# A three-layer network on one Trainium2 core: modulation, attention masks and forgetting bias moved from TensorE to VectorE

## What is computed

```python
def masked_softmax(s, mask):
    s = jnp.where(mask, s, -jnp.inf); m = max(s); e = where(mask, exp(s - m), 0.0)
    return e / where(sum(e) > 0, sum(e), 1.0)

# layer 0: stick-breaking attention (8 heads) beside sparse attention (8 heads, 2 key groups)
for each query block i of 128:                      # nsa_attention
    pc = masked_softmax(q_i @ kc.T * scale, cmp_end <= tpos)        # 31 compressed keys
    ps = masked_softmax(q_i @ k_slc.T * scale, kpos <= tpos)        # selected keys
    pw = masked_softmax(q_i @ k_win.T * scale, causal, window 512)
    o  = gate0 * pc @ vc + gate1 * ps @ v_slc + gate2 * pw @ v_win

# layer 1: forgetting attention (16 heads)
cum = cumsum(log_sigmoid(f + b_f))
s = q_i @ k.T * scale + (cum[query] - cum[key]);  p = masked_softmax(s, key <= query)

# both layers end with a gated feed-forward
a, b = split(h @ w_in); a = conv3(a) + conv_b; x = x + (silu(a) * b) @ w_out      # 2 x 2816 features

# second network: six modulation vectors for c and for c_ctx
sh1, sc1, g1, sh2, sc2, g2 = split(silu(c) @ ada_w + ada_b, 6)                    # ada_w is 1024 x 6144
csh1, csc1, ...            = split(silu(c_ctx) @ ada_w + ada_b, 6)
h = rmsnorm_2(x, norm1_g) * (1 + sc1) + sh1
# then neighbourhood attention, spatial gating, a merge, a product-key expert layer
```

## Time and profile before

| | before |
|---|---|
| median of 3 runs | 3334.88 us |
| lowest, highest | 3329.38, 3342.94 us |
| the profiled execution | 3336.33 us |
| its span | 3334.9 us |
| its mean granted TensorE clock | 0.968 |
| TensorE busy | 3136.4 us (94% of the span) |
| VectorE busy | 2149.3 us (64%) |
| ScalarE busy | 1283.5 us (38%) |
| GpSimd busy | 810.8 us (24%) |
| HBM read | 476.42 MB |

### The profile page before, as it was taken

The page is one execution under the profiler, slowest core; times in us unless marked ns, Lnnn a source line. Parts: engine busy times, 40 slices in busy tenths (PEclk is TensorE's granted clock), DMA queues, the critical chain, the costliest instruction groups (busy, mean ns, idle before and its releaser), DMA issues. The chain is left out here.

```text
span 3334.9 us, 44712 instructions
## 1 busy us (share of the span) xinstructions
PE 3136.4 (94%) x17144; PEld 2684.2 (80%) x17144; DVE 2149.3 (64%) x4042; ACT 1283.5 (38%) x2260; POOL 810.8 (24%) x708
## 2 busy tenths in 40 slices
PE   7998899999999999997998989888989999999998
PEld 5556678888776788885776768888989999999998
DVE  4464556465566563644334348997878888888886
ACT  3344543233343332333442223338943433333333
POOL 1001110000000300024000023578824333433431
PEclk9799999999999999997998989999999999999999
DMA  3441113222211223221111222454699989999893
GB/s 140 145 159 66 39 64 104 93 95 101 70 52 51 89 91 105 95 95 43 51 61 64 95 76 84 131 192 169 233 331 315 330 307 323 323 325 337 305 327 115
DMA packets 182690, 516.03 MB, mean 155 GB/s; under 512 B 15056, under 2 KB 77520, under 8 KB 177360
## 3 DMA queue, kind: packets, MB, share of 16 engines
q1 hardware_dynamic: 129344, 307.27, 26.9%
q0 software_dynamic: 40464, 160.45, 13.8%
q10 hardware_dynamic: 12672, 45.47, 3.6%
HBM read 476.42 MB, written 36.70 MB: 154 GB/s over the span
## 5 line engine op out<-in xcount | busy, mean ns | idle before, releaser
L238 PE MATMUL bank<-h_hi,w_hi 128*128 128x512 f32 (+1 forms) x2528 | 963.6, 381 | 67.6 <-DVE h_lo L304 13.7
L238 PE MATMUL bank<-h_lo,w_hi 128*128 128x512 f32 (+1 forms) x2528 | 949.7, 376 | 0.0
L212 DVE TENSOR_TENSOR w_lo<-w_raw,w_hi 128x1024 fp32r<-128x1024 f32 (+1 forms) x460 | 590.0, 1283 | 318.5 <-ACT w_hi L206 316.3
L206 ACT ACTIVATE w_hi<-w_raw 128x1024 fp32r<-128x1024 f32 (+1 forms) x508 | 546.0, 1075 | 529.1 <-PE bank L238 511.3
L238 PEld LDWEIGHTS bank<-h_hi,w_hi 128*128 128x128 f32 x2528 | 484.4, 192 | 152.9 <-issue 50.0
L238 PE MATMUL bank<-h_hi,w_lo 128*128 128x512 f32 (+1 forms) x2528 | 596.6, 373 | 9.5 <-POOL w_lo L219 9.5
L238 PEld LDWEIGHTS bank<-h_lo,w_hi 128*128 128x128 f32 x2528 | 485.6, 192 | 65.5 <-issue 10.2
L238 PEld LDWEIGHTS bank<-h_hi,w_lo 128*128 128x128 f32 x2528 | 460.1, 189 | 75.5 <-POOL w_lo L219 10.5
L238 PE MATMUL bank<-e_hi,w_hi 128*128 128x384 f32 x1024 | 345.5, 337 | 9.1 <-DVE e_lo L2369 9.1
L238 PE MATMUL bank<-e_lo,w_hi 128*128 128x384 f32 x1024 | 344.2, 336 | 0.0
L2278 POOL DMA_INDIRECT own_row<-in_u_rows,own_e x128 | 156.8, 1225 | 300.2 <-DVE sums L2406 261.1
(11 more groups left out here) (434 smaller groups left out, 4326.2 us busy)
## 6 DMA issues: line engine op xcount, KB each, us to landing
w_raw<-in_w SPq DMA_DIRECT2D x476, 512.0 KB, 3.8
ada_w<-in_ada_w POOLq DMA_DIRECT2D x24, 1024.0 KB, 5.1
expert_weights<-G ACTq DMA_DIRECT2D x12, 2048.0 KB, 7.2
Gin<-expert_weights SPq DMA_DIRECT2D x32, 768.0 KB, 9.2
w_raw<-in_w SPq DMA_DIRECT2D x32, 704.0 KB, 4.1
hidden_ahead<-u_stage ACTq DMA_DIRECT2D x48, 192.0 KB, 3.0
ahead<-hidden_ahead SPq DMA_DIRECT2D x24, 384.0 KB, 6.5
x<-in_x ACTq DMA_DIRECT2D x4, 512.0 KB, 10.7
```

Source lines behind the costliest of these rows:

```text
L206: sc.activation(w_hi[s][:, 0:n], w_raw[raw_slot[u]][:, 0:n], ACT.Copy).then_inc(*w_hi_made.next(u))
L212: ve.tensor_tensor(w_lo[s][:, 0:n], w_raw[raw_slot[u]][:, 0:n], w_hi[s][:, 0:n], ALU.subtract).then_inc(*w_lo_made.next(u))
L238: m = te.matmul(out, wt, moving, start=(not low and k == 0 and moving is hi), stop=(low and k == len(blocks) - 1))
```

## The change

1. **Modulation** leaves TensorE and the sparse attention. A new function `modulation` is part of each feed-forward layer: 24 tiles of 128 x 1024 of the transposed `ada_w` per layer, fetched by GpSimd (512 KB each, a ring of four), and for each tile two VectorE row products, with silu(c) and with silu(c_ctx), each summed along its row into `mod`. The host lays `ada_w` out by output row, and c and c_ctx as rows repeated over the partitions; ScalarE fetches these (1 MB) and takes their Silu once per layer. In the first half the products begin with the third feature tile, one product ahead of `a_in` and one ahead of `bn`, then one beside each out unit; in the second half all 11 tiles have two. `scaled_g` is made at the end of the second layer.
2. **Masks of the sparse attention.** The mask matmuls are gone. VectorE adds `near` or `cfar` to the scores and takes the minimum in one instruction (`tensor_tensor_reduce`), which writes the masked scores to `Pm`; the exponential reads them there. Scores of slot g wait for that minimum of slot g-1. Transposes are those of slot g-2, VectorE does the reciprocal and scaling of slot g-1 after the minimum of slot g, and the query unit's matmuls stand between scores and transposes.
3. **Bias of the forgetting attention.** The `pick` matmuls are gone. The running sum is written to memory by GpSimd and read back repeated over the partitions, two rows per pair (512 KB, a ring of four `crow`). VectorE adds it and takes the minimum in one instruction; queries carry -scale.

```diff
@@ ffn, vector()
+            products = products_vector()
                     split_lo(ub)
+                    if half or f >= 2:
+                        run(products, 1)
...
                     ve.scalar_tensor_tensor(cv[0][:, :], a_in[:, 2:T + 2], tap[2], cv[1][:, :], ALU.mult, ALU.add).then_inc(*dve.next(name, "conv", half, f))
+                    if half or f >= 2:
+                        run(products, 1)
                     ve.wait_ge(*w_used.at(ub))
@@ modulation, products_vector()
+            ve.wait_ge(*act.at("silu c", layer))
+            for n in tiles:
+                ve.wait_ge(*tile_in[n % RING].at(n))
+                if n - 1 in tiles:
+                    ve.wait_ge(*dve.at("ada first", n - 1))
+                ve.scalar_tensor_tensor(spent[:, :], w[n % RING][:, :], 1.0, silu[:, 0, :], ALU.mult, ALU.mult,
+                                        accum_out=mod[:, n, 0:1]).then_inc(*dve.next("ada first", n))
+                yield
+                ve.wait_ge(*dve.at("ada first", n))
+                ve.scalar_tensor_tensor(w[n % RING][:, :], w[n % RING][:, :], 1.0, silu[:, 1, :], ALU.mult, ALU.mult,
+                                        accum_out=mod[:, n, 1:2]).then_inc(*dve.next("ada", n))
+                yield
@@ nsa, tensor()
                         if g:
-                            te.wait_ge(*act.at("nsa exp", hh, g - 1))
+                            te.wait_ge(*dve.at("nsa least", hh, g - 1))
...
-                        te.matmul(part, ident_r[:, :], mask, start=False, stop=True).then_inc(*pe.next("nsa scores", hh, g))
...
-                if 0 < g <= slots and g % 2 == 0:
-                    ada_turn(g // 2 - 1)
-                for n in range(2) if g == 1 else (g,) if 1 < g < slots else ():
-                    ada_tensor(n)
@@ nsa, vector()
-                        least = ve.tensor_reduce(sm[:, k + 1:k + 2], S[:, 0:w], AX.X, ALU.min)
...
+                        far = cfar[:, i, :] if b == 0 else near[:, T - w:T]
+                        ve.tensor_tensor_reduce(Pm[hh][m % 2][b][:, 0:w], s_bank[hh][:, 0:w], far, 1.0, 1e20,
+                                                ALU.add, ALU.min, sm[:, k + 1:k + 2]).then_inc(*dve.next("nsa least", hh, g))
@@ fox, tensor()
                         if m:
-                            te.wait_ge(*act.at("fx exp", hh, m - 1))
...
-                        te.matmul(S[:, 0:kw], pick[rows, p, :], cum_hi[rows, 0:kw], start=False, stop=False)
-                        te.matmul(S[:, 0:kw], pick[rows, p, :], cum_lo[rows, 0:kw], start=False, stop=True).then_inc(*pe.next("fx scores", hh, m))
+                            te.wait_ge(*dve.at("fx least", hh, m - 1))
@@ fox, vector()
+                        if i == 0:
+                            ve.wait_ge(*crow_in[p % 4].at(p))
                         ve.wait_ge(*dve.here())
-                        row_max(S[:, 0:kw], small[hh][:, c:c + 1], small[hh][:, c + 1:c + 2], SCALE).then_inc(*dve.next("fx max", hh, m))
+                        ve.tensor_tensor_reduce(Pm[hh][m % 2][:, 0:kw], S[:, 0:kw], crow[p % 4][:, hh, 0:kw], 1.0, 3e38,
+                                                ALU.add, ALU.min, small[hh][:, c + 1:c + 2]).then_inc(*dve.next("fx least", hh, m))
@@ fox, gpsimd()
+            gp.wait_ge(*dve.at("fx cum"))
+            gp.dma_start(cum_dram[:, :], cum[0:16, :]).then_inc(*cum_out.next("out"))
+            gp.wait_ge(*cum_out.at("out"))
             for p in range(8):
...
+                if p >= 4:
+                    gp.wait_ge(*dve.at("fx least", 1, 4 * (p - 3) - 1))
+                gp.dma_start(crow[p % 4][:, :, :], cum_dram[2 * p:2 * p + 2, :].unsqueeze(0).to_broadcast([P, 2, T])).then_inc(*crow_in[p % 4].next(p))
```

238 lines of the change are left out of this document (103 added, 135 removed).

## The result

| | before | after |
|---|---|---|
| median, runs | 3336.07 us, 4 | 3253.95 us, 4 |
| lowest, highest | 3329.38, 3342.94 | 3249.13, 3254.31 |
| ratio to before, 95% interval | | 0.9745, 0.9725 to 0.9765 |
| span of the profiled execution | 3334.9 | 3252.7 |
| mean granted TensorE clock | 0.968 | 0.971 |

The account below looks back on a forecast made before the run. TensorE, busy 94% of the span, was taken as the bound. Terms of -52.6 (sparse attention), -10 (forgetting attention) and +6 (feed-forward) sum to -56.6: from 3336.3 to 3279.7, less 1.5 for the median, 3278 us; range 3254 to 3309.

Parts of the forecast that it names:

- The sparse attention core: Term for taking modulation and masks off TensorE in the sparse attention: -52.6 us, from -67.6 to -35.4.
- I take 10: Sparse attention core: 10 us of VectorE's work stay exposed over its 48 slots, between bounds of 0 and 22.
- 3 x 30.3: Sparse attention core: the first three head pairs take 30.3 us each after the change, down from 44.28.
- Low clock, 5 of 10.2 us kept: Sparse attention core: 10.2 us were lost to low clock early on before the change, and 5 of them stay.
- The matmuls taken out, 14.0 per pair: Sparse attention core: TensorE loses 10.6 us of modulation and 3.4 us of masks in each head pair.
- The scores of a slot no longer wait for the exponential: Sparse attention core: scores wait for the earlier minimum instead, shortening the loop through the score bank; no gain was counted.
- The forgetting attention: Term for bias matmuls off TensorE: 10.6 us saved over 32 steps, 0.4 lost at the start; -10, from -13 to -6.
- The feed-forward layers: Term for row products on VectorE, mostly fitting its idle: +6 us, 3 for out units, 3 for late tiles; 0 to +16.
- The 3 us for the first out units: Feed-forward layers: the first out unit after each of 4 halves waits 0.75 us for the last tile's differences.
- the probabilities staying in the chain: Rival: VectorE's 30 us wait for ScalarE's exponential in the sparse attention core stays on the path; 3308 us, chance 0.12.
- The second: Rival: slow row products make VectorE the bound of the feed-forward layers; at twice the time 3368 us, chance 0.03.
- a low clock through a thinned core: Rival: TensorE's clock falls to half over the whole sparse attention core; 3377 us, chance 0.03.

Follow-up runs that it names:

- mod_only: The kernel before with only the modulation moved to the feed-forward layers, masks and forgetting bias left on TensorE; 3327.21 us, ratio 0.9965.
- wait_exp: The changed kernel with scores of slot g again waiting for the exponential of slot g-1, not the minimum; 3292.76 us, ratio 0.9862.
- fox_only: The kernel before with only the forgetting attention's bias moved to VectorE; 3326.13 us, ratio 0.9961.
- probs_first: The changed kernel with VectorE's old order, reciprocal and scaling of slot g right after the minimum of slot g; 3271.37 us, ratio 0.9804.
- masks_only: The kernel before with only the masks moved to VectorE and the new slot order, modulation kept in the slots; 3302.34 us, ratio 0.9878.
- masks_both: The changed kernel with the 96 mask matmuls put back on TensorE beside VectorE's additions; 3260.94 us, ratio 0.9769.
- no_products: The changed kernel with the modulation's row products cut to their first column, so results are wrong and only time counts; 3251.87 us, ratio 0.9742.
- fill_start: The changed kernel with nine matmuls of the next query unit taken ahead of slot 0, into TensorE's first wait; 3249.54 us, ratio 0.9729.
- more_vector: The changed kernel with one more VectorE operation of 0.43 us in each slot of the sparse attention core; 3265.80 us, ratio 0.9783.

## Why the prediction was wrong

The direction and the place were right. The size was not, and it was one term, the sparse attention core; in it failed the 10 us put down for an exposed VectorE, the price of the first pair, and a wait priced at nothing.

**The sparse attention core (-52.6 forecast, -70.6 measured).** Its steps:
- *"I take 10" for VectorE exposed.* TensorE's idle in the third pair is 0.77 us, 1.19 before the change, so nothing stood there. This is the largest part of the error. My own sign, a third pair of some 33 us and scores that end near 218, was missed: 29.61 and 198.5.
- *3 x 30.3: the first pair priced as a full one.* Its trace has 166 matmuls where the third has 218, since the first slots have no transposes and values yet. It takes 27.78 us, 6.8 of them at half clock, so some 24.4 at full clock (an estimate), 5.9 less than 30.3.
- *Low clock, 5 of 10.2 us kept.* 10.2 us of the core stand at half clock, worth some 5: this allowance was right in size. But the 10.2 that I took as before's loss was too small for the same reason as the pair's price: 34.1 us stood at half clock, worth some 17.
- *The matmuls taken out, 14.0 per pair.* Measured as differences of third pairs at full clock: the modulation 38.56 - 29.61 = 8.95 where I counted 10.6, the masks 2.2 where I counted 3.4. The start-to-start differences of the earlier trace rows overstated both, by 2.8 us a pair together.
- *"The scores of a slot no longer wait for the exponential ... that shortens the loop through the score bank."* I wrote it down and priced it at nothing, because TensorE's waits in the core before looked small. As a mechanism this is the step that failed. The new order with its waits is worth 44.28 - 40.8 = 3.5 us a pair (an estimate) while the modulation is there, and with the old wait most of the modulation's gain would not have come (`mod_only`, `wait_exp`). That the third pair came out at 29.6 against the 30.3 of my matmul count is luck: these two errors cancel.
- The fourth pair took 25.0 where I had 23.6, of which the 3.4 us at half clock explain 1.7. I read its 37.58 before from the transposes of slot 45; to those behind the last scores it is 35.2, and the end is longer by the same 2.4. By my own marks the end took 2.0 off where I had 1.5.

So of the 18 us missing 10 are VectorE, 5.9 the first pair, 1.4 the second and third at 0.7 each, and the rest the fourth and the end.

**The forgetting attention (-10 forecast).** 7.9 in this trace, 11.6 in that of `fox_only`, 11 at full clock. The first minimum does wait for the sums to come back, for 1.54 us:

```profile
805.45 0.29 DVE L1475 CUSTOM_DVE_ANT_0 fx_p<-bank,fx_crow 128x128 f32<-128x128 f32 x1 [1.54 <-DMA fx_crow<-fox_cum]
```

The first step takes 7.1 us from scores to scores against 5.8 before, but that wait is not the reason. TensorE is busy in all of it, at a clock of 0.76, as the stretches of this step and the next show:

```profile
803.02:810.13 7.11, 7.11 (x25) 5.41 (x26) 3.15 (x11) 1.93 (x5) 0.00 (x0) 0.76 0.61 235
810.13:816.63 6.50, 6.50 (x33) 4.46 (x32) 4.18 (x12) 2.37 (x7) 0.00 (x0) 1.00 0.24 82
```

`probs_first` has a like wait, 1.2 us, and full clock, and there the step takes 5.5 us.

**The feed-forward layers (+6 forecast, +2.0 measured).** The product price of 1.218 us was exact, and 2.60 us of work did fit into 2.63 us of idle. The 3 us for the first out units did not appear. The late tile of the second layer was real, but it cost 1.1 us, not 3.

**Outside my terms.** 2.5 us ahead in the projections and 4.0 in the expert layer belong to no edit. In the projections between 40 and 80 us the granted clock is 0.96 in before's trace and 1.00 in the changed kernel's, and 0.91 to 1.00 in those of the experiments. In the expert layer one wait of TensorE for ScalarE's first conversion of a block, which hangs on a transfer out of memory, is 9.16 us in before and 5.24 in the changed kernel:

```profile
2362.17 0.69 PE L238 MATMUL bank<-h_hi,w_hi 128*128 128x384 f32 x1 [5.24 <-ACT w_hi L206]
```

masks_only, which touches nothing there, has gained the same 4 us at that place. My range had no room for such things: its low end was just the sum of the good ends of three terms. That the time fell outside it comes from the sparse attention, 3.0 us beyond the good end of its term, and these 6.5.

**The rivals.** The first, the probabilities staying in the chain, fell: VectorE's idle on the exponential went from 30.5 to 0.3 us. Its mechanism is real, though: `probs_first`, which undoes that overlap, costs 17 to 20 us. The second fell with the products at 1.218 us. Where the Trainium skill (Vector Engine (DVE) Microarchitecture Reference, "Points that are easy to get wrong") halves such an instruction, this trace has it at 1.22 us for 1024 elements, the same as the plain subtraction w_lo of the same size in the earlier trace rows; no halving against that instruction shows. The third, a low clock through a thinned core, did not come in the changed kernel (0.95) but did in `mod_only`, where the waits on ScalarE were left in: 75.1 of 166.0 us at half clock. I had priced it at 0.03 and tied it to shorter pieces with more waits. In these runs the kernels with the most idle are mostly those with the most time at half clock; `masks_both` and the two traces of before's code don't fit that.

## What to carry to other kernels

Work taken off the busiest engine is gained only as far as no wait was hidden behind it: before you count it, follow who frees the bank that the next instruction needs, and price the loop without the cover. Here the modulation's move alone gained 14 us in its stage, the masks' with the new order 28, and both together 71; one wait on the exponential instead of the minimum took 39 of them back. Read the granted clock of each version beside its idle time, since a few us of waiting can go with many more at half clock. Price work by leaving it out at full clock, not by start-to-start differences alone, which overstated it by a fifth (modulation) to a half (masks) here.

## What the runs showed of the hardware

- TensorE's granted clock goes to 0.5 about 1 us behind a wait of 1.6 us at the start of the core. In three traces of the same code (the changed kernel twice, `no_products`) it stays there 6.8, 6.8 and 3.4 us; with nine matmuls in that wait (`fill_start`) the first pair stays at 1.00. In the code of before it stayed there 27.3 us in one trace and 41.0 in another, in part with TensorE recorded busy throughout.
- In `mod_only`, `wait_exp` and `more_vector` more waits in the core went with more low clock, and by the estimate above the clock cost as much or more. Without the modulation's cover (`mod_only`) TensorE was idle 9.4 us more and stood at half clock 41 us more. One more VectorE operation of 0.43 us a slot (`more_vector`) added 5.6 us of idle and 23.9 at half clock.
- Traces of unchanged code differ by 2 us in the projections (the changed kernel's two), 7.2 in the sparse attention (before, `fox_only`), up to 5.7 in the forgetting attention and 4 in the expert layer. In both attentions it is the time at half clock that differs. An effect under some 7 us in one stage needs that stage's rows at full clock, not the total.
